# Block 2's modulation units move from the recurrences' stage to the differential attention's

## What is computed

```python
# first_block, layer 0 and 1
mod = (silu(c) @ ada_w[l] + ada_b[l]);  mod_c = (silu(c_ctx) @ ada_w[l] + ada_b[l])
sh1, sc1, g1, sh2, sc2, g2 = split(mod, 6)           # the same of mod_c
h  = rms_norm(x, norm_mix_g) * (1 + sc1) + sh1
y  = even_layer_mixer(h, ...)     # layer 0: hgrn2 recurrences (two directions, 4 heads)
                                  #   and differential attention (4 heads, q over 256 + 256 keys)
x  = x + g1 * y;  x = x + g2 * routed_moe(...)       # 16 experts
# second_block: the modulations of block 2
mod_x = (silu(c_2) @ w_mod_2 + b_mod_2);  mod_c = (silu(c_ctx_2) @ w_mod_2 + b_mod_2)
```

## Time and profile before

| | us |
|---|---|
| median of 3 runs | 3331.49 |
| lowest, highest | 3328.1, 3333.6 |
| the profiled execution | 3330.94 |
| its span (first to last instruction) | 3329.5 |
| mean granted TensorE clock | 0.889 |
| TensorE, VectorE, ScalarE busy | 2723.8, 1289.7, 852.0 |
| recurrences | 158 to 385 |
| differential attention | 505 to 566 |

### The profile page before, as it was taken

The page is one execution under the profiler, slowest core; times in us unless marked ns, Lnnn a source line. Parts: engine busy times, 40 slices in busy tenths (PEclk is TensorE's granted clock), DMA queues, the critical chain, the costliest instruction groups (busy, mean ns, idle before and its releaser), DMA issues.

```text
span 3329.5 us, 28245 instructions
## 1 busy us (share of the span) xinstructions
PE 2723.8 (82%) x11331; PEld 1566.9 (47%) x11331; DVE 1289.7 (39%) x2075; ACT 852.0 (26%) x1292; POOL 105.6 (3%) x172
## 2 busy tenths in 40 slices
PE   6988596859999898799958777759969897878776
PEld 3744574647777777446522222215446443222222
DVE  3376738358888887424320000023364113000001
ACT  2322323147777776112100000012212111000000
POOL 0011200010000000100010000000000000000000
PEclk8989798879999999795769999978989997999998
DMA  8399460169999995610169999981201333899997
GB/s 300 121 353 385 143 230 1 52 227 342 362 353 353 351 347 215 219 42 1 39 258 400 399 403 398 407 313 61 84 0 56 126 139 115 337 410 409 409 409 283
DMA packets 296077, 820.06 MB, mean 246 GB/s; under 512 B 11075, under 2 KB 11241, under 8 KB 295680
## 3 DMA queue, kind: packets, MB, share of 16 engines
q1 hardware_dynamic: 275840, 753.87, 59.8%
q0 software_dynamic: 14512, 46.28, 4.0%
q10 hardware_dynamic: 5584, 17.98, 1.4%
HBM read 780.20 MB, written 37.90 MB: 246 GB/s over the span
## 4 chain that ended last, share of the span: by engine, by line
PE 58%; DMA 22%; DVE 13%; issue 3%; ACT 2%; SPq 1%; POOL 1%; PEldq 0%; DVEq 0%; ACTq 0%; POOLq 0%
PE PS L245 55%; DMA ring<-in_moe_w_up 7%; DMA ring<-in_w_e_up 4%; DMA ring<-in_w_e_down 3%; DMA ring<-in_moe_w_gate 3%; DVE cut L398 3%; DMA ring<-in_w_e_gate 2%; ACT cut L390 1%; PE PS L2137 1%; DMA ring<-in_moe_w_down 1%; PE PS L1644 1%; DMA ring<-in_ada_w 1%; SPq L360 1%; DVE xeT L1653 1%; DVE hgrn L874 0%
## 5 line engine op out<-in xcount | busy, mean ns | idle before, releaser
L398 DVE TENSOR_TENSOR cut<-ring,cut 128x1024 fp32r<-128x1024 f32 x424 | 505.8, 1222 | 229.8 <-ACT cut L390 214.3
L390 ACT CAST cut<-ring 128x1024 fp32r<-128x1024 f32 x424 | 439.8, 1049 | 318.9 <-PE PS L245 291.3
L245 PE MATMUL PS<-cut,xeT 128*128 128x512 f32 x1536 | 361.2, 393 | 10.1 <-DVE cut L398 10.1
L245 PEld LDWEIGHTS PS<-cut,xeT 128*128 128x128 f32 x1536 | 286.9, 189 | 75.4 <-issue 16.3
L245 PE MATMUL PS<-ring,xeT 128*64 128x512 f32 x1024 | 244.9, 627 | 67.6 <-DMA ring<-in_moe_w_gate 36.6
L245 PE MATMUL PS<-ring,hidT 128*64 128x512 f32 (+1 forms) x1024 | 243.4, 626 | 68.5 <-DMA ring<-in_w_e_down 30.4
L245 PE MATMUL PS<-ring,XE 128*32 128x512 f32 x1008 | 244.6, 639 | 57.9 <-DMA ring<-in_w_e_up 36.8
L245 PE MATMUL PS<-cut,hidT 128*128 128x512 f32 x768 | 194.6, 412 | 41.8 <-DVE hidT L1653 41.8
L245 PE MATMUL PS<-HT,ring 128*128 128x512 f32 (+2 forms) x576 | 206.9, 527 | 0.7 <-DVE HT L482 0.7
L245 PEld LDWEIGHTS PS<-ring,xeT 128*64 128x64 f32 x1024 | 78.3, 143 | 232.6 <-issue 172.5
L245 PEld LDWEIGHTS PS<-cut,hidT 128*128 128x128 f32 x768 | 149.9, 198 | 77.4 <-DVE hidT L1653 45.6
(11 more groups left out here) (517 smaller groups left out, 2891.2 us busy)
## 6 DMA issues: line engine op xcount, KB each, us to landing
ring<-in_moe_w_gate SPq DMA_DIRECT2D x64, 2048.0 KB, 11.7
ring<-in_moe_w_up SPq DMA_DIRECT2D x64, 2048.0 KB, 10.3
ring<-in_moe_w_down SPq DMA_DIRECT2D x64, 2048.0 KB, 12.2
ring<-in_w_e_up SPq DMA_DIRECT2D x32, 2048.0 KB, 18.4
ring<-in_w_e_down SPq DMA_DIRECT2D x32, 2048.0 KB, 19.9
ring<-in_w_e_gate SPq DMA_DIRECT2D x31, 2048.0 KB, 18.4
ring<-in_ada_w SPq DMA_DIRECT2D x24, 2048.0 KB, 12.9
ring<-in_w_in SPq DMA_DIRECT2D x13, 2048.0 KB, 7.7
```

The source lines that it names most:

```text
L245: return pe.matmul(o, l, r, start=start, stop=stop, **kw)
L390: act.copy(self.bufs[i % len(self.bufs)][0], w).then_inc(self.high.sem, 1)
L398: dve.tensor_tensor(low, w, high.bitcast(F32), ALU.subtract).then_inc(self.low.sem, 1)
```

## The change

The 12 pieces of block 2 (`ada2`) go behind `in` 4 to 7 in the ring's order. Units 6 and 7 leave the recurrences' turns on all engines and GpSimd's queue there, and become a last stage of `staggered` in the differential attention: one turn of `mod_tensor`, `mod_vector` and `mod_scalar` at each iteration from i = 5 on (7 turns a unit), their GpSimd part behind the meeting after projection b. For them bank 7 serves both the column-group sums and the closing sum, so the attention's output stays in bank 6 alone and a new group of four waits for the copy of the last. They get a place of their own for their tiles. The waits for the stores change: the norm after the recurrences waits for unit 5's, GpSimd's reload of the gates for unit 3's, and the square root behind the attention for unit 7's.

```diff
--- before.py
+++ after.py
@@ -265,9 +265,9 @@
         W.add(("in", n), cols(win, 512 * n), "dve")
     add_ada("ada0", ada[0], range(2, 6))
     add_ada("ada1", ada[1], range(6))
-    add_ada("ada2", I["w_mod_2"][0], range(6))
     for n in range(4, 8):
         W.add(("in", n), cols(win, 512 * n), "dve")
+    add_ada("ada2", I["w_mod_2"][0], range(6))
     for n in range(2):
         W.add(("wo", n), cols(wo, 512 * n), "dve")
     for e in range(16):
@@ -524,7 +524,7 @@
     allc = (0, 1, 2, 3)
 
 
-    mod_place = {u: room("mod_place", 1536, 0 if u < 2 else 12032) for u in (0, 2)}
+    mod_place = [room("mod_place", 1536, at) for at in (0, 12032, 17152)]
     MODS = []
     for tag, half, bias, gains, dst, js in (
             ("ada0", 0, I["ada_b"][0], ((2, I["norm_mix_g"][0]), (8, I["norm_ffn_g"][0])), None, range(2)),
@@ -544,8 +544,12 @@
     mod_out = S.new("mod_out", "act_q", 16)
 
     def mod_tiles(u):
-        place = mod_place[0 if u < 2 else 2]
+        place = mod_place[0 if u < 2 else 1 if u < 6 else 2]
         return place[:, 0:512], place[0:12, 512:1024], place[0:6, 1024:1536]
+
+    def mod_banks(u):
+
+        return (bank(6), bank(7)) if u < 6 else (bank(7), bank(7))
 
     def mod_gpsimd(u):
         _, _, bias, gains, _, _, h = MODS[u]
@@ -565,14 +569,15 @@
     def mod_tensor(u):
         tag, half, _, _, _, js, h = MODS[u]
         sums, _, br = mod_tiles(u)
+        acc, added = mod_banks(u)
         for j in js:
             w, n = piece((tag, j, h))
             pe.wait_ge(*landed(n))
             if j == js[0] and u:
-                pe.wait_ge(*mod_taken(u - 1))
+                pe.wait_ge(*(mod_taken if u < 6 else mod_done)(u - 1))
             for c in range(8):
                 q = c % 4
-                last = mm(bank(6)[32 * q:32 * q + 32, :], CP[:, half, c, 10 - 2 * j:42 - 2 * j], w[:, c, :],
+                last = mm(acc[32 * q:32 * q + 32, :], CP[:, half, c, 10 - 2 * j:42 - 2 * j], w[:, c, :],
                           j == js[0] and c < 4, j == js[-1] and c > 3, skip_group_check=True)
             last.then_inc(used.sem, 1)
             yield
@@ -580,8 +585,8 @@
         pe.wait_ge(*mod_in(mod_loads[u + 1] - 1))
         if u:
             pe.wait_ge(*mod_done(u - 1))
-        mm(bank(7)[0:12, :], KC[:, C_SUM:C_SUM + 12], sums, True, False)
-        mm(bank(7)[0:12, :], KC[0:6, C_REP:C_REP + 12], br, False, True).then_inc(mod_summed.sem, 1)
+        mm(added[0:12, :], KC[:, C_SUM:C_SUM + 12], sums, True, False)
+        mm(added[0:12, :], KC[0:6, C_REP:C_REP + 12], br, False, True).then_inc(mod_summed.sem, 1)
         yield
 
     def mod_vector(u):
@@ -590,10 +595,11 @@
         for _ in js:
             yield
         dve.wait_ge(*consumed(W.at[tag, js[-1], h]))
-        dve.tensor_copy(sums, bank(6)).then_inc(mod_taken.sem, 1)
+        acc, added = mod_banks(u)
+        dve.tensor_copy(sums, acc).then_inc(mod_taken.sem, 1)
         o = MOD[:, 512 * h:512 * h + 512] if dst is None else GB
         dve.wait_ge(*mod_summed(u))
-        dve.scalar_tensor_tensor(out=o, in0=bank(7)[0:12, :], scalar=KC[0:12, C_ONE:C_ONE + 1], in1=GB,
+        dve.scalar_tensor_tensor(out=o, in0=added[0:12, :], scalar=KC[0:12, C_ONE:C_ONE + 1], in1=GB,
                                  op0=ALU.add, op1=ALU.mult).then_inc(mod_done.sem, 1)
         yield
 
@@ -1006,12 +1012,12 @@
             yield
 
     def mods(one):
-        for u in range(2, 8):
+        for u in range(2, 6):
             yield from one(u)
 
     def hgrn_gpsimd():
         after_meeting(pool, 1)
-        for u in range(2, 8):
+        for u in range(2, 6):
             mod_gpsimd(u)
 
     hgrn_gpsimd()
@@ -1038,7 +1044,7 @@
 
     def onorm_scalar():
         act.dma_start(HT.rearrange("p c t -> p (c t)"), HD).then_inc(ht_in.sem, 16)
-        act.wait_ge(*mod_out(5))
+        act.wait_ge(*mod_out(3))
         act.wait_ge(*sq_summed(0))
         act.activation(ss, ss, ACT.Sqrt).then_inc(sq_rooted.sem, 1)
 
@@ -1062,7 +1068,7 @@
 
     def onorm_gpsimd():
         after_meeting(pool, 2)
-        pool.wait_ge(*mod_out(5))
+        pool.wait_ge(*mod_out(1))
         pool.dma_start(MOD[4:12, :], M0[4:12, :]).then_inc(mod_back.sem, 16)
 
     onorm_scalar()
@@ -1227,7 +1233,20 @@
                 if stage and 0 <= i - k < n:
                     stage(i - k)
 
+    after_project = met[pe].n
+
+    def late_mods(one):
+        for u in (6, 7):
+            yield from one(u)
+
+    def diff_gpsimd():
+        after_meeting(pool, after_project)
+        for u in (6, 7):
+            mod_gpsimd(u)
+
     def diff_tensor():
+        late = late_mods(mod_tensor)
+
         def scores(u):
             qi, h = divmod(u, 4)
             k0, nk = keys_of(qi)
@@ -1252,14 +1271,15 @@
             qi, h = divmod(u, 4)
             k0, nk = keys_of(qi)
             pe.wait_ge(*(even_taken, odd_taken)[u % 2](u // 2))
-            if h == 0 and qi > 1:
-                pe.wait_ge(*y_taken(qi - 2))
+            if h == 0 and qi:
+                pe.wait_ge(*y_taken(qi - 1))
             for j in range(nk // P):
-                last = mm(bank(6 + qi % 2)[:, h * P:(h + 1) * P], aT[u % 2][:, j * P:(j + 1) * P],
+                last = mm(bank(6)[:, h * P:(h + 1) * P], aT[u % 2][:, j * P:(j + 1) * P],
                           VA[:, k0 // P + j, h * P:(h + 1) * P], j == 0, j == nk // P - 1)
             last.then_inc(valued.sem, 1)
 
-        staggered(16, scores, None, None, turn, values)
+        staggered(16, scores, None, None, turn, values, lambda u: next(late, None))
+        all_of(late)
 
     def diff_scalar():
         def exps(u):
@@ -1278,7 +1298,10 @@
                     act.wait_ge(*valued(u - 2))
                 act.copy(aT[1][:, 0:nk], bank(5)[:, 0:nk]).then_inc(odd_taken.sem, 1)
 
-        staggered(16, exps, None, None, take)
+        late = late_mods(mod_scalar)
+        staggered(16, exps, None, None, take, None, lambda u: next(late, None))
+        all_of(late)
+        act.wait_ge(*mod_out(5))
         act.wait_ge(*sq_summed(0))
         act.activation(ss, ss, ACT.Sqrt).then_inc(sq_rooted.sem, 1)
 
@@ -1313,10 +1336,12 @@
         def keep(u):
             if u % 4 == 3:
                 dve.wait_ge(*valued(u))
-                dve.tensor_copy(YB[:, u // 4, :], bank(6 + u // 4 % 2)).then_inc(y_taken.sem, 1)
+                dve.tensor_copy(YB[:, u // 4, :], bank(6)).then_inc(y_taken.sem, 1)
 
         dve.wait_ge(*sub_in(0))
-        staggered(16, maxima, None, mix, take, keep)
+        late = late_mods(mod_vector)
+        staggered(16, maxima, None, mix, take, keep, lambda u: next(late, None))
+        all_of(late)
         dve.wait_ge(*y_taken(3))
         for c in allc:
             vs.add(dve.tensor_tensor(Pm[0][c], YB[:, c, :], YB[:, c, :], ALU.mult))
@@ -1334,6 +1359,7 @@
                 dve.scalar_tensor_tensor(out=YC[:, c, sl], in0=YB[:, c, sl], scalar=ss[:, 4 * c + h:4 * c + h + 1], in1=sub,
                                          op0=ALU.mult, op1=ALU.mult)
 
+    diff_gpsimd()
     diff_tensor()
     diff_scalar()
     diff_vector()
```

## The result

The changed kernel takes 3345.94 us (median of 5 runs, 3340.53 to 3348.83) against 3328.10 beside it: a ratio of 1.0045 [1.003, 1.0059], about 15 us slower (17.8 by these medians). Two repeats on other occasions gave 3346.51 against 3332.01, 1.0045 [1.0031, 1.0059], and 3344.68 against 3329.78, 1.0046 [1.0032, 1.006]. The forecast was slower by 7.3 us, 3338.2, with a range to 3347. The direction held. The size was half of what came. The profiled execution took 3340.53 us (span 3339.0).

A forecast was written before the change was run, and what follows sets the result against it. VectorE, TensorE and transfers together bound the recurrences, VectorE the differential attention. Terms -15.1 + 21.1 + 1.3 = +7.3 us on 3330.94 gave 3338.2 us; range 3329 to 3347, +2 to +14 likely.

The forecast's parts named there:

- The recurrences, -15.1: Recurrences without units 6 and 7: 12.3 us from the turns plus 2.8 from a tail saved, bounds 12.3 to 18.1.
- The two tails: Ends of recurrence steps 1 and 2: the first stays slow, the second turns fast at the upper clock, saving 2.8 us.
- What the units cost there: Recurrences, steps 1 to 3: 61.60 us with units, 49.30 without; 12.3 saved, since VectorE needs what TensorE needs in level turns.
- The attention, +21.1: Differential attention: TensorE becomes the bound, 26.3 us new work plus 2.1 waits less 7.35 idle; bounds 19.0 to 28.4.
- the transfers and the single bank hide: Attention: pieces land in time with 4.7 us cover, and waits for the single output bank's 0.69 us copy cost nothing.
- the hand-off at iteration 11: Attention, unit 6's sum: two VectorE copies of 0.69 us each precede the closing product, which ends at 553.6 us.
- The root, +1.3: ScalarE's square root behind the attention: behind two waits its table load starts late, costing 1.3 us, bounds 0 and 1.3.
- a change later than 631 us: Stages after 631 us: none expected to change; one there would be an effect the forecast had missed.
- A: Attention iterations 5 to 17: products fit beside VectorE's work, only the sums' hand-offs cost 9.2 us; -4.6, 3326.3 us; chance 0.14.
- B: Attention: transfers set the end at 7.6 us a piece, the last landing 8.2 us late; +15.5, 3346.4 us; chance 0.12.
- C: Recurrences and attention nearly cancel: both tails at upper clock, -18.1, attention loss 19.0; about +1, 3332 us; chance 0.12.

The follow-up runs named there:

- The delayed gain: Kernel before the change, with the closing gain of units 2 to 7 one turn later in the recurrences: 3315.20 us, 0.9957.
- half the products: Changed kernel with only 4 of the 8 products of each piece of units 6 and 7, all transfers and sums kept: 3336.57 us, 1.0014.
- the delayed hand-offs: Changed kernel with the closing gain one turn later for units 2 to 5 in the recurrences and 6 and 7 in the attention: 3336.57 us, 1.0016.

## Why the direction was right and the size too small

**The recurrences, -15.1.** Measured -13.9 as a mean of three traces each; the stretch without units took 47.53 us where 49.30 had been taken over from step 3. The two tails were neither one slow (15.7) and one fast (12.9) but 13.92 and 13.87 at a granted clock of 0.88, nearly the same sum. The saving of the first pair alone would be 17.1, because the first trace of the kernel before had the longest recurrences of the three. This term was right within its bounds. That it came within 1.2 us is in part luck: it was read from one trace, and the stage itself differs by 3.5 us between traces of the kernel before and by 2.9 between those of the changed one.

**What the units cost there** was named wrongly. The forecast let 12.3 us stand as what was left when level turns need both engines alike. The delayed gain shows that the larger part was VectorE waiting for the closing sum, 21.9 us over six units. In the stretch from which the term was read, in the kernel before:

```profile
297.29 0.74 DVE L596 SCALAR_TENSOR_TENSOR mod_place<-PS,KC,mod_place 12x512 f32<-12x512 f32 x1 [4.24 <-PE PS L245]
...
328.17 0.74 DVE L596 SCALAR_TENSOR_TENSOR mod_place<-PS,KC,mod_place 12x512 f32<-12x512 f32 x1 [3.17 <-PE PS L245]
```

These two waits are 7.4 of the 12.3 us, VectorE's own copies and gains 2.9; the other 2.0 aren't split further. The wrong name didn't spoil the sum, since the difference of two stretches holds whatever causes it, but it hid the better change.

**The attention, +21.1.** Measured 72.60 - 49.41 = 23.2 in the first trace and 24.1 in the second. That TensorE becomes the bound, that an iteration takes its summed work, that the transfers and the single bank hide, all were as forecast (half the products; no ring wait; 0.6 us uncovered). The term was mis-sized by 2 to 3 us, at the hand-off at iteration 11. TensorE waited 2.42 us there instead of 1.4, and the costs at full clock didn't hold behind that wait: from start to start the sum took 0.85 more, the scores 0.5, the turn 0.2, the values 0.45 and the piece 1.2, together 3.2 us. Turn and values behind one another were a little cheaper than taken (4.39 an iteration, not 4.6), which gave back 1.4 us ahead of the hand-off. Counted from the first scores, piece 5 ended at 39.9 us where the forecast has 41.3, the closing sum at 47.1 (46.8), the last piece at 68.4 (66.2) and the last output copy at 72.6 (70.6). The second trace's 0.9 us more come from the opening of the stage, where the granted clock was 0.50 for 12 us instead of about 4.

**The root, +1.3.** As forecast: 1.62 - 0.28 = 1.34, undone by moving one wait. Load (1.28 us) and root (0.22) stand directly behind one another within the 1.62 us; the Trainium skill's 2.66 for a switch of sets ("ScalarE: Activation LUTs", What ACT_TABLE_LOAD costs) isn't in the trace.

**The sum.** With the measured terms it is -13.9 + 23.5 + 1.3 = +10.9, 3.6 over the forecast. The spans add 2.2 more: the routing's later clock (+1.2), the steps behind the last scatter (+0.8), and small differences ahead of the recurrences (+0.7) and in the output projection (-0.6). All of this the forecast had put at nothing, and it had named a change later than 631 us as one that it would have missed. **What stays open** is whether the routing's step is scatter. Counted from the router's load to the last scatter it takes 62.6 us in 6 of the 8 traces of kernels with units in the attention (59.9 and 60.0 in the others), and 58.9 to 59.6 in the 5 without. The clock shows how it happens; why it should happen more often there isn't shown, and 6 of 8 against 0 of 5 leaves room for an effect of the change, some 3 us where it comes. The medians differ by 14.5 to 17.8 us, the spans of the traces by 13; with an interval of +10 to +20 us these agree.

**Rivals.** A fell by the half products and by the delayed hand-offs, B by the changed kernel's own waits. C's near cancelling didn't occur: neither of its ends was met.

## What to carry to other kernels

Idle transfers in a stage say nothing of the engine that has to multiply what they bring: add the moved work to that engine's own per iteration and compare with the pace, here 2.71 + 1.86 against 3.35 us. Where two engines hand a small result back and forth inside one turn of interleaved queues, let each do its part in a turn of its own before moving the work elsewhere: that brought 14 us, the move cost 15. It did so in a stage that VectorE paces; in the attention, which TensorE paces, the same delay took 1 to 2 us off the stretch. And look at the clock behind a wait of a busy TensorE: the 2.42 us of the hand-off were followed by 3.2 us of slower products.

## What the runs showed of the hardware

A TensorE wait of 2.4 us, after 24.5 us in which it was busy throughout at a granted clock of 1.00, was followed by products at 1.4 to 1.8 times their time at the upper level (sum 2.83 for 1.98, piece 3.11 for 1.92, scores 1.23 for 0.70), with 0.50 granted from 535 to 541 us. In all eight traces with units in the attention a wait of 2.2 or 2.4 us at this hand-off was followed by such products; behind a wait of 1.38 us, with both delays, the sum took its 1.98 us. No run took the 2.4 us wait away, so that it brings the lower level is what the traces suggest and not shown by an experiment. Without any change of kernel, later stages differ by steps of 3 to 5 us by when TensorE returns to 2.4 GHz (0.93 or 0.76 granted in the same 20 us). And ScalarE's table load stood behind its waits where two preceded the root, and ahead where one did: 1.3 us for one line's place.
